# Second block of a two-block transformer kernel: VectorE and ScalarE issue scores, convolution and tile rounding ahead of weight splitting, embedding statistics and sigmoid

## What is computed

```python
h = rms_norm(x, g_mix);  proj = h @ w_in                 # latents, dq, dk, dv, sq, sk, sv, gate logits
# 24 attention items (heads): 8 differential, 8 windowed, 8 latent
s = q @ k.T + slope * distance;  p = softmax(s);  o = p @ v
x = x + (sum(sigmoid(gates[b]) * (o[b] @ w_branch[b]) for b in range(3))) @ w_out
h = rms_norm(x, g_ffn)
a = depthwise_conv(h @ w_ffn_gate, conv_w, conv_b)       # 3 taps along the tokens
x = x + (gelu(a) * (h @ w_ffn_up)) @ w_ffn_down          # hidden width 2816 = 22 tiles of 128
e = rms_norm(pe @ w_ple_proj, g_ple)                     # the embedding
x = x + sigmoid(rms_norm(x, g_ple_in) @ w_ple_gate) * e
```

## Time and profile before

| | |
|---|---|
| median of three runs | 1714.12 us (1710.3 to 1717.04) |
| the profiled execution | 1718.73 us, of which its span 1716.9 us |
| PE busy | 1643.5 us, 96% of the span |
| PEld, DVE, ACT, POOL busy | 87%, 68%, 54%, 26% |
| second block, layer 0 and layer 1 | about 750 to 1236 us and 1236 to 1717 us of the span |
| distance of the two layers at the attention start (first DVE scores) | 482.2 us (823.92 and 1306.12) |
| mean granted TensorE clock | 0.981 of full speed |

### The profile page before, as it was taken

One profiled execution on the slowest core, in us unless ns is written; L12 is line 12 of the kernel. 1 busy time (PEld: TensorE's weight loads), 2 busy tenths in 40 slices (PEclk: granted clock), 3 DMA queues, 4 the chain that ended last, 5 costly groups with the idle time before them and its releaser, 6 DMA issues.

```text
span 1716.9 us, 30143 instructions
## 1 busy us (share of the span) xinstructions
PE 1643.5 (96%) x11354; PEld 1495.4 (87%) x11354; DVE 1172.6 (68%) x1601; ACT 921.4 (54%) x1576; POOL 446.3 (26%) x184
## 2 busy tenths in 40 slices
PE   8989999999999999999999999999899999999997
PEld 6778799988887899978899989998788999889996
DVE  5677754557776654476884877767767856777677
ACT  5664544446644544465655564445755555554445
POOL 2212222212222222234511122222235311222222
PEclk9989999999999999999999999999999999999999
DMA  8432466646423655556333455655554333466653
GB/s 330 161 117 99 138 209 194 195 161 211 154 80 116 231 186 189 190 168 207 118 105 105 142 197 182 222 184 179 180 199 147 110 101 116 163 219 193 214 185 128
DMA packets 82564, 288.74 MB, mean 168 GB/s; under 512 B 9052, under 2 KB 11909, under 8 KB 81925
## 3 DMA queue, kind: packets, MB, share of 16 engines
q1 hardware_dynamic: 77352, 272.58, 48.4%
q10 hardware_dynamic: 5084, 14.37, 2.5%
HBM read 284.81 MB, written 2.11 MB: 167 GB/s over the span
## 4 chain that ended last, share of the span: by engine, by line
PE 60%; DVE 8%; ACT 3%; issue 2%; DVEq 0%; ACTq 0%
PE bank L721 28%; PE bank L738 25%; DVE w_lo L687 2%; PE bank L1295 2%; PE bank L1276 1%; ACT w_hi L683 1%; PE bank L1267 1%; PE bank L766 1%; PE bank L1255 1%; PE bank L775 0%; PE bank L1308 0%; DVE qk L2529 0%; PE bank L1187 0%; PE bank L911 0%; DVE z L2503 0%
## 5 line engine op out<-in xcount | busy, mean ns | idle before, releaser
L687 POOL TENSOR_TENSOR w_lo<-raw,w_hi 128x1024 fp32r<-128x1024 f32 x146 | 380.1, 2604 | 1159.5 <-ACT w_hi L683 1159.5
L687 DVE TENSOR_TENSOR w_lo<-raw,w_hi 128x1024 fp32r<-128x1024 f32 x364 | 561.7, 1567 | 152.5 <-ACT w_hi L683 150.4
L683 ACT ACTIVATE w_hi<-raw 128x1024 fp32r<-128x1024 f32 x510 | 519.9, 1052 | 97.7 <-PE bank L738 44.1
L721 PE MATMUL bank<-x_t_hi,w_hi 128*128 128x256 f32 x1984 | 320.7, 284 | 5.1 <-ACT gl L1431 2.7
L721 PE MATMUL bank<-x_t_hi,w_lo 128*128 128x256 f32 x1984 | 310.4, 279 | 0.0
L721 PE MATMUL bank<-x_t_lo,w_hi 128*128 128x256 f32 x1984 | 309.7, 278 | 0.0
L721 PEld LDWEIGHTS bank<-x_t_hi,w_hi 128*128 128x128 f32 x1984 | 273.8, 191 | 17.8 <-issue 5.7
L721 PEld LDWEIGHTS bank<-x_t_hi,w_lo 128*128 128x128 f32 x1984 | 267.2, 190 | 0.0
L721 PEld LDWEIGHTS bank<-x_t_lo,w_hi 128*128 128x128 f32 x1984 | 265.6, 190 | 0.0
L738 PE MATMUL bank<-w_hi,x_t_hi 128*128 128x512 f32 (+3 forms) x448 | 134.3, 383 | 9.6 <-issue 5.8
L738 PE MATMUL bank<-w_hi,x_t_lo 128*128 128x512 f32 (+3 forms) x448 | 131.7, 377 | 1.9 <-DVE x_t_lo L1963 1.9
(11 more groups left out here) (390 smaller groups left out, 2082.1 us busy)
## 6 DMA issues: line engine op xcount, KB each, us to landing
raw<-stream SPq DMA_DIRECT2D x511, 512.0 KB, 4.3
rows<-rows ACTq DMA_DIRECT2D x4, 1024.0 KB, 4.7
gain<-rows ACTq DMA_DIRECT2D x8, 512.0 KB, 3.9
hv_p<-hv_dram ACTq DMA_DIRECT2D x14, 256.0 KB
x<-x_in SPq DMA_DIRECT2D x2, 512.0 KB, 5.1
bias_r<-rev_dram SPq DMA_DIRECT2D x1, 1024.0 KB, 7.4
hv_dram<-hv ACTq DMA_DIRECT2D x2, 512.0 KB, 7.7
y_out<-x SPq DMA_DIRECT2D x2, 512.0 KB, 2.7
```

What stands on the lines that cost most here:

```text
L683: self.eng.activation(w_hi[:, i, :], raw[:, i, :], ACT.Copy).then_inc(hi_done.sem, 1)
L687: self.eng.tensor_tensor(w_lo[:, i, :], raw[:, i, :], w_hi[:, i, :].bitcast(F32), ALU.subtract).then_inc((lo_pool if self.part == "pool" e ...
L721: mm = pe.matmul(target, a[:, i, w0 + kt * P:w0 + (kt + 1) * P], b[:, k0 + kt, :], start=kt + k == 0, stop=k == 2 and kt == kts - 1)
```

## The change

Five pieces of order are changed, all in the second block. No instruction is added but two table-set loads by name (`preload_act_table_set`), and none is removed.

1. Attention start, DVE: `item(0)` and `item(1)` go ahead of the splitting that follows sq3, the scaling of the window keys goes between them, and `split.ahead(uid["skv3"])` comes after both.
2. Feed-forward, DVE: at step 0 only the units up to down0 are split ahead of the first convolution (before: up to down1); step 1 catches up.
3. Feed-forward, ACT: the two sums of squares of e move from ahead of the loop into steps 1 and 2, logarithm and exponential into step 3, with a load of their table set there. The scaling of e on DVE moves from step 4 to step 6.
4. Layer seam, ACT: the next layer's first tile is rounded ahead of `embedding_gate(1)`, with the sigmoid set loaded first.
5. Layer seam, DVE: that tile's remainder is taken ahead of `embedding_added(2)`.

```diff
@@ ScalarE, second_block
                 split.ahead(uid["gate0"])
-                for t in range(T):
-                    act.wait_ge(*banks.read(at, f"pp{t}"))
-                    step(act.activation(sq2[:]..., e[:, t, :], ACT.Square, accum_out=stat[:, 16 + t:17 + t]))
-                step(act.activation(stat[:, 16:18], stat[:, 16:18], ACT.Ln, bias=eps6[:], scale=1.0 / D))
-                act.activation(stat[:, 18:20], stat[:, 16:18], ACT.Exp, scale=-0.5).then_inc(c["ple_rstd"].sem, 1)
                 for i in range(FT):
...
                     act.activation(hs2_hi[:, i % TAIL, :], hs2[:, i % 2, :], ACT.Copy).then_inc(c["h_hi"].sem, 1)
+                    if i in (1, 2):
+                        act.wait_ge(*banks.read(at, f"pp{i - 1}"))
+                        step(act.activation(sq2[:]..., e[:, i - 1, :], ACT.Square, accum_out=stat[:, 15 + i:16 + i]))
+                    if i == 3:
+                        act.preload_act_table_set("natural_log_exp_and_others")
+                        step(act.activation(stat[:, 16:18], stat[:, 16:18], ACT.Ln, bias=eps6[:], scale=1.0 / D))
+                        act.activation(stat[:, 18:20], stat[:, 16:18], ACT.Exp, scale=-0.5).then_inc(c["ple_rstd"].sem, 1)
...
                     split.upto(N2 + 4)
+                    act.preload_act_table_set("sigmoid_and_others")
+                    round_tile(after, "xt", 0, 0)
                     embedding_gate(1)
                     act.preload_act_table_set("natural_log_exp_and_others")
-                    round_tile(after, "xt", 0, 0)
                     rms_stats(after, 0, 1)
@@ VectorE, second_block
                 head_scale(at, "sq", 3, 8, 0, sqn)
-                split.ahead(uid["skv3"])
                 head_means(at, 4, 2)
-                head_scale(at, "skv", 4, 2, 2, skn)
...
                     if i < MLA and i % 2 == 0:
                         item(i)
+                        if i == 0:
+                            head_scale(at, "skv", 4, 2, 2, skn)
                         item(i + 1)
+                        if i == 0:
+                            split.ahead(uid["skv3"])
...
                 for i in range(FT):
-                    split.ahead(uid[f"up{i}"])
-                    if i == 4:
+                    if i:
+                        split.ahead(uid[f"up{i}"])
+                    else:
+                        split.upto(uid["down0"] + 1)
+                    if i == 6:
                         dve.wait_ge(*c["ple_rstd"](at, 1))
...
                     split.upto(N2 + 4)
+                    rest_of_tile(after, "xt", 0, 0)
                     embedding_added(2)
-                    rest_of_tile(after, "xt", 0, 0)
                     embedding_added(3)
```

More of the change, by code:

```diff
@@ L1860, in second_block @@
                 split.ahead(uid["gate0"])
-                for t in range(T):
-                    act.wait_ge(*banks.read(at, f"pp{t}"))
-                    step(act.activation(sq2[:].rearrange("p t n -> p (t n)"), e[:, t, :], ACT.Square,
-                                        accum_out=stat[:, 16 + t:17 + t]))
-                step(act.activation(stat[:, 16:18], stat[:, 16:18], ACT.Ln, bias=eps6[:], scale=1.0 / D))
-                act.activation(stat[:, 18:20], stat[:, 16:18], ACT.Exp, scale=-0.5).then_inc(c["ple_rstd"].sem, 1)
                 for i in range(FT):
@@ L1876, in second_block @@
                     act.activation(hs2_hi[:, i % TAIL, :], hs2[:, i % 2, :], ACT.Copy).then_inc(c["h_hi"].sem, 1)
+                    if i in (1, 2):
+                        act.wait_ge(*banks.read(at, f"pp{i - 1}"))
+                        step(act.activation(sq2[:].rearrange("p t n -> p (t n)"), e[:, i - 1, :], ACT.Square,
+                                            accum_out=stat[:, 15 + i:16 + i]))
+                    if i == 3:
+                        act.preload_act_table_set("natural_log_exp_and_others")
+                        step(act.activation(stat[:, 16:18], stat[:, 16:18], ACT.Ln, bias=eps6[:], scale=1.0 / D))
+                        act.activation(stat[:, 18:20], stat[:, 16:18], ACT.Exp, scale=-0.5).then_inc(c["ple_rstd"].sem, 1)
                 act.wait_ge(*c["conv_ready"](at, FT))
```

## The result

Over 20 executions of each kernel the changed one takes 1720.88 us (median, 1714.46 to 1725.51) and the one before 1715.01 us (1710.08 to 1718.65): ratio **1.0036**, 95% interval 1.0026 to 1.0045 (the intervals of the other ratios below are meant so too). That is 6.2 us slower, within the 0.5% that the forecast called no change, and 5.6 us were forecast. The profiled execution took 1720.76 us, its span is 1718.9 us at a mean granted clock of 0.985.

What follows compares the result with a forecast made beforehand. PE was taken as the bound, busy 96% of the span, so order pays only where PE stands still. Feed-forwards +6.0, attention +1.3 and seam -1.7 gave +5.6: 1719.7 us for the median, range 1705 to 1728.

Steps and rivals of the forecast that it cites:

- Feed-forward: Each layer's feed-forward: down0's wait becomes four small ones, losing 2.2 us, taken as 3.0 with the clock, 6.0 together.
- The starts of H: Start of each feed-forward step's rounded product; from step 3, predicted to make down3 to down6 late by 1.1, 2.1, 0.2, 2.8.
- the clock behind the last new wait: Feed-forward, ahead of down6: the 2.8 us wait may drop the clock, 1.7 us on top; 3.0 taken instead of 2.2.
- Attention start of layer 0: Three splits beside POOL push item(2) 2.7 us later; layer 0 loses 0.8, plus 1.0 for the clock.
- Layer 1's: Attention start of layer 1: a gain of 1.5 us, less 1.0 taken for the clock.
- Seam: Between the layers: PE restarts at 1226.4 instead of 1228.78, tile 1 then waits for its norm; -1.7 us, ends -2.5 and 0.
- +5.6: Whole kernel: sum of feed-forward +6.0, attention +1.3 and seam -1.7 us.
- PE's waits in steps 3 to 6: Feed-forward: sign that the prediction is wrong if these waits sum to under 4 us.
- DVE wins the ports: First rival, feed-forward and attention: DVE wins or shares ports with POOL, splits take 1.2 us; 1699.3 us, chance 0.15.
- every new wait above 2 us drops the clock: Second rival, feed-forwards, attention and seam: slow clock at the worst place; +11, 1725.1 us, chance 0.27.
- waits only trade places: Third rival, whole kernel: time comes out within 2 us of before, 1714; chance 0.18.
- The missing Square: Feed-forward steps 1 and 2: Square not in gelu's set, more loads, adding 5.1 us; counted with the second rival, chance 0.27.

Runs made afterwards that it cites:

- e13_changed_behind_splits: Changed kernel with only ACT's sums of squares, logarithm and exponential moved behind their step's roundings, ahead of the convolution wait; 1712.93 us, ratio 0.9993 to the kernel before.
- e10_behind_splits: Kernel before with the short step 0; ACT's work on e behind the roundings in steps 1, 2 and 5, DVE's scaling in step 9; 1706.05 us, ratio 0.9933.
- e1_attention: Kernel before with piece 1 of the change alone (attention start, DVE); 1718.55 us, ratio 1.0033.
- e3_seam: Kernel before with pieces 4 and 5 of the change alone (layer seam); 1713.33 us, ratio 0.9991.
- e12_all_orders: Kernel before with the attention order of e5_attention_spread, the feed-forward order of e10_behind_splits and the seam's pieces 4 and 5; 1698.05 us, ratio 0.9892.
- e9_combined: Kernel before with the attention order of e5_attention_spread, the feed-forward order of e8_embedding_at_slack and the seam's pieces 4 and 5; 1706.89 us, ratio 0.9937.
- e2_feed_forward: Kernel before with pieces 2 and 3 of the change alone (feed-forward); 1720.02 us, ratio 1.0038.
- e5_attention_spread: Kernel before, attention start alone: units up to gl2 split ahead of head_means 4, key scaling between item(0) and item(1), three splits behind item(3); 1706.03 us, ratio 0.9933.
- e4_late_embedding: e2_feed_forward with the work on e later: squares in steps 9 and 10, root in 12, scaling in 14, gain's load in 17; 1716.07 us, ratio 1.0019.
- e8_embedding_at_slack: Kernel before with pieces 2 and 3, but squares behind products of steps 6 and 7, root behind 8, scaling in 16, gain's load in 17; 1714.63 us, ratio 0.999.
- e6_memset: Changed kernel with POOL writing zeros instead of its remainders, its units' low parts left out of the result; 1678.41 us, ratio 0.9774.

## Why the prediction was right, and where its terms were not

**Feed-forward: mechanism right, the term too large (3.0 us predicted, 1.4 measured, twice).** The starts of H predicted were 1021.8, 31.0, 39.8, 49.5, 59.8, 68.3 and 79.3; measured, less the 0.53 us by which this execution was late at the first gate unit, 1021.7, 30.6, 39.1, 48.8, 59.2, 67.6 and 78.6. From step 3 on every period was right within 0.1 us (9.7 at step 3, 10.3 at step 4, 11.0 at step 6). The failing terms are small: steps 1 and 2 are each 0.3 us shorter, and a product starts 0.46 us behind H (1059.71 to 1060.18), not 0.67. These 0.9 us come off the 2.2. The third, 0.8 us, was the clock behind the last new wait: down6 is late by 2.8 us, as predicted (2.37 of it are idle time in the profile), and the clock stayed at 1.00 both times. By how late each product starts (its distance from the one before, less 8.21), steps 3 to 6 have 0.3, 2.1, 0.2 and 2.8 us where 1.1, 2.1, 0.2 and 2.8 were predicted, 5.4 in all for 6.2. The places, steps 3, 4 and 6 and none after, were right, and e13_changed_behind_splits and e10_behind_splits show the cause that the prediction named. What it didn't see is the way out: ACT's idle time, which it used only to hide the gelu load, would have hidden all of ACT's part.

**Attention start of layer 0: the work right, the clock too small (1.8 predicted, 3.1 measured).** Shifted by the 2.6 us between the executions, item(0), item(2), the turn of item 1 and the weighing of item 0 came at 820.2, 830.7, 831.6 and 833.9 where 820.2, 830.9, 831.7 and 834.0 were predicted. gl3 came at 837.3, not 835.7. Behind the waits of 2.33 and 1.70 us PE worked at half clock up to the first matmuls of gl3, and that cost 2.3 us, the upper end of my term, not 1.0. e1_attention and e13_changed_behind_splits, with the same order, have 2.9 and 3.1 us here.

**Layer 1's** was predicted at -0.5 and came at -0.2.

**Seam: -1.7 predicted and seen, but only for 10 us.** Tile 1's turn came 1.75 us earlier. The 1.9 us in which PE idles, which I had noted as no more than a widening of the range, dropped the clock (0.80; it was 1.00 at this place before), and the projections gave 1.4 back. The net is -0.3. e3_seam and e13_changed_behind_splits repeat it, and in e12_all_orders the clock is 0.79 there too; in e9_combined it held. So what was wrong in this term is the clock, whose cost the prediction's sum put at nothing: in four of the five profiles with this order it fell.

So +5.6 met 5.4 by the traces because one term too large (feed-forwards, by 3.2 in all) stood against two too small (attention by 1.6, seam by 1.4). The near hit of the number is therefore luck in part; the mechanisms of the feed-forward and of the attention start are not. In the prediction's own list of what would make it wrong, PE's waits in steps 3 to 6 must not be under 4 us: they sum to 5.4 by the lateness in which the 6.2 was worked out, and to just 4 (1.65 and 2.37) by idle time.

**The rivals.** That DVE wins the ports: not so; splits take 3.7 and 5.66 us, each ending behind POOL's. That every new wait above 2 us drops the clock: it did in attention, not in the feed-forwards of this execution, so neither "each" nor "none"; in e2_feed_forward, with the same feed-forward order, it fell once in each layer. That waits only trade places: no, 1.0026 is the lower end of the interval, 4.5 us, and this rival stays within 2. The missing Square: no load stands ahead of it, so it lies in gelu's set.

## What to carry to other kernels

Work that is moved on an engine with idle time can cost nothing or nearly all of itself, by its place within the step (here 4.2 us of ACT's work made 4.0 us a feed-forward, or none): look for the instruction in front of which the engine waits, and put it there, not behind the one that others wait for. Room gained by starting earlier does not accumulate without end; here it is capped by the seven slots of the weight ring and has a second due date at the end of the loop, where the consumer runs through what the producer left. And a long run of work moved ahead of a short one leaves a hole where it stood: fill that hole in the same edit.

## What the runs showed of the hardware

**Behind a wait of about 2 us the clock falls in some executions and holds in others.** Ahead of down0 PE waited 1.90 us in four feed-forwards of e1_attention and e3_seam; the clock of the next 8 us was 0.79 in three and 1.00 in one. After 2.31 and 2.40 us in the kernel before it was 0.79, after 2.30 us in e5_attention_spread 1.00, twice:

```profile
1022.00:1030.00 8.00, 8.00 (x59) 7.49 (x59) 5.91 (x10) 5.16 (x7) 2.49 (x1) 1.00 0.68 224
1499.60:1507.60 8.00, 7.93 (x56) 7.46 (x57) 5.91 (x9) 5.39 (x7) 2.50 (x1) 1.00 0.64 210
```

After waits of 2.50 and 2.48 us (e4_late_embedding) it fell, after 2.52 us, twice in e8_embedding_at_slack, once. Over all profiles but that of e6_memset the feed-forwards have 19 single waits of 1.8 to 2.6 us, and the clock fell behind 12. At the seam it fell behind 1.8 to 1.9 us in four of five, and behind the old wait of 3.12 us in all eight. In the attention start of the changed order, where a second wait follows, it fell in all six. Behind the attention start's old waits of 1.3 to 1.7 us it fell in five of twelve; in e8_embedding_at_slack it was 0.79 and 1.00, in e10_behind_splits 0.79 and 0.57, layer 0 first. After single waits of 1.65, 1.2 and 1.3 us in the stretches above it did not fall.

The trace of the kernel before could have told that length alone does not decide. At two places outside the change the clock held behind a wait of 2.57 us and fell behind one of 1.67 us, the last being at the end of the attention, behind small matmuls (L775):

```profile
744.70:752.70 8.00, 6.78 (x34) 5.29 (x35) 6.67 (x10) 5.42 (x11) 0.00 (x0) 1.00 0.07 14
945.28:953.28 8.00, 7.70 (x53) 7.47 (x54) 5.55 (x11) 6.09 (x12) 0.00 (x0) 0.80 0.07 25
```

Each fall in the feed-forwards, at the seam and in attention cost 1.4 to 2.3 us. As an estimate from these, with two of three waits followed by a fall of some 2 us, a wait of about 2 us is worth its length and another 1.3 us.

**A matmul has two speeds at full clock.** In two of the feed-forwards each matmul of the gate and up products took 281 ns instead of 276, all through the loop, with a granted clock of 1.00 and the same code: in layer 1 of e5_attention_spread, and in layer 0 of e3_seam. Its matmuls (min, median, max ns), layer 0 and then layer 1 of e5_attention_spread:

```profile
L721 PE MATMUL bank<-x_t_hi,w_lo x20: 276/276/281, 1053.9 to 1062.4; 128*128 128x256 f32 x20
...
L721 PE MATMUL bank<-x_t_hi,w_lo x20: 281/281/281, 1540.9 to 1549.7; 128*128 128x256 f32 x20
```

A step is then 8.42 us instead of 8.21. The two feed-forwards of e5_attention_spread, alike otherwise, differ by 3.8 us for it. In these two it starts at down0; the 281 ns also stand in short stretches elsewhere, as in the gate and up products of one step of the changed kernel (1071.4 to 1076.5). I can't say what decides it; it may be part of why single executions of one kernel lie up to 10 us apart.

**A table load** took 1.28 us in each row above, and it started as soon as ACT was idle, also where the function itself still waited: the load at 1059.92 in e10_behind_splits, which stands at gelu's own line (L1874) and which no line of the kernel names, ran 2.4 us ahead of its gelu. That is why two loads fit into one idle stretch there.
